# Two projection units on the unnormalised input, with the root put to them when they leave PSUM

## The reference

```python
xf = xf * lax.rsqrt(jnp.mean(xf * xf, axis=-1, keepdims=True) + EPS)   # rmsnorm
xn = (xf * g)
proj = xn @ w_in
q, k, v, u, gates = jnp.split(proj, splits, axis=-1)
...
bu = einsum('blgc,gpc->blgp', u, bb)        # state-space layer on u: a scan over the tokens
y = C x + d_skip * u
```

## Time and profile before

| | before |
|---|---|
| median of 3 runs | 1391.95 us (1390.6 to 1392.52) |
| the profiled execution | 1393.16 us |
| its span, first to last instruction | 1391.3 us |
| PE busy | 1369.7 us, 98% of the span |
| DVE, ACT, POOL busy | 49%, 60%, 15% |
| mean DMA rate | 182 GB/s |

### The profile page before, as it was taken

How to read it: one execution, slowest core, us unless ns; L and a number is a source line. 1 busy time by engine, 2 the same in 40 slices (tenths; PEclk the granted TensorE clock), 3 DMA queues, 4 the chain that set the end, 5 groups by cost and what they waited for, 6 DMA issues and landing times.

```text
span 1391.3 us, 18289 instructions
## 1 busy us (share of the span) xinstructions
PE 1369.7 (98%) x6634; PEld 1109.9 (80%) x6634; DVE 685.4 (49%) x1317; ACT 832.3 (60%) x1211; POOL 205.3 (15%) x240
## 2 busy tenths in 40 slices
PE   7999999999999999999999999999999999999998
PEld 4888877777788888888888887777798888888887
DVE  6993378988644445554154154745255301213324
ACT  7554877778665666665365366665667654535443
POOL 1111111100011111111111111110111111111112
PEclk9999999999999999999999999999999999999999
DMA  9998776676688888888878886755668898887973
GB/s 298 217 175 210 182 189 148 144 165 140 142 205 214 195 185 196 192 190 194 207 185 185 185 212 163 167 137 121 144 168 189 182 211 185 198 195 180 211 166 91
DMA packets 85670, 252.67 MB, mean 182 GB/s; under 512 B 16720, under 2 KB 24016, under 8 KB 85584
## 3 DMA queue, kind: packets, MB, share of 16 engines
q0 software_dynamic: 32400, 116.93, 46.8%
q1 hardware_dynamic: 51344, 131.06, 30.9%
q10 hardware_dynamic: 1840, 3.54, 0.7%
HBM read 126.98 MB, written 3.41 MB: 94 GB/s over the span
## 4 chain that ended last, share of the span: by engine, by line
PE 90%; DVE 5%; DMA 2%; ACT 2%; issue 1%; DVEq 0%; ACTq 0%
PE pg L646 26%; PE pg L648 25%; PE pg L647 25%; PE py L920 1%; PE ps L840 1%; PE ps L815 1%; PE ps L816 1%; PE ps L817 1%; DMA w_lo<-w_raw 1%; PE ps L1105 1%; PE ps L1113 1%; DMA act_lo<-w_raw 1%; DVE pairs L1842 1%; PE py L1123 1%; DVE acc L1845 0%
## 5 line engine op out<-in xcount | busy, mean ns | idle before, releaser
L646 PE MATMUL pg<-x_hi,w_hi 128*128 128x512 f32 x1008 | 397.5, 394 | 1.3 <-DVE gates L1842 1.3
L648 PE MATMUL pg<-x_hi,w_lo 128*128 128x512 f32 x1008 | 392.6, 390 | 0.0
L647 PE MATMUL pg<-x_lo,w_hi 128*128 128x512 f32 x1008 | 392.4, 389 | 0.0
L604 POOL DMA_DIRECT2D w_lo<-w_raw x221 | 190.9, 864 | 1144.5 <-ACT w_lo L1236 1068.3
L1235 ACT ACTIVATE w_hi<-w_raw 128x1024 fp32r<-128x1024 f32 (+1 forms) x215 | 224.4, 1044 | 108.9 <-PE pg L648 92.6
L646 PEld LDWEIGHTS pg<-x_hi,w_hi 128*128 128x128 f32 x1008 | 189.2, 188 | 49.9 <-issue 11.9
L1236 ACT ACTIVATE w_lo<-w_raw 128x1024 fp32r<-128x1024 f32 (+1 forms) x215 | 223.2, 1038 | 0.0
L648 PEld LDWEIGHTS pg<-x_hi,w_lo 128*128 128x128 f32 x1008 | 189.2, 188 | 39.9
L647 PEld LDWEIGHTS pg<-x_lo,w_hi 128*128 128x128 f32 x1008 | 189.3, 188 | 39.3 <-issue 1.0
L646 PE MATMUL pg<-act_hi,w_hi 128*128 128x512 f32 x424 | 164.9, 389 | 0.0
L647 PE MATMUL pg<-act_lo,w_hi 128*128 128x512 f32 x424 | 164.9, 389 | 0.0
(11 more groups left out here) (457 smaller groups left out, 1923.3 us busy)
## 6 DMA issues: line engine op xcount, KB each, us to landing
w_raw<-weights SPq DMA_DIRECT2D x218, 512.0 KB, 4.8
w_lo<-w_raw POOLq DMA_DIRECT2D x213, 512.0 KB, 5.6
kq_rot<-kq_raw SPq DMA_DIRECT2D x64, 64.0 KB, 2.4
w_raw<-weights SPq DMA_DIRECT2D x8, 384.0 KB, 4.3
w_lo<-w_raw POOLq DMA_DIRECT2D x8, 384.0 KB, 4.7
hid<-x SPq DMA_DIRECT2D x4, 512.0 KB, 5.6
hid<-x ACTq DMA_DIRECT2D x8, 256.0 KB, 5.0
act_lo<-w_raw POOLq DMA_DIRECT2D x4, 512.0 KB, 7.9
```

The source lines that it names most:

```text
L604: pool.dma_start(low_of(u)[:, 0:n], w_raw[:, s, 0:n], accum_op=ALU.add).then_inc(lo_in[s], 16)
L646: pe.matmul(bank[:], wh, xh(k), start=n == 0, stop=False)
L647: pe.matmul(bank[:], wh, xl(k), start=False, stop=False)
L648: last = pe.matmul(bank[:], wl, xh(k), start=False, stop=n == len(ks) - 1)
```

## The change

Units 0 and 1 are multiplied with the halves of x times norm weight, without the root (`raw_hi` by ACT, `raw_lo` by DVE), as each tile of x lands; the sum of squares runs on PE between and behind unit 0's products. The root is multiplied to the two outputs by DVE when they leave PSUM, in place of ACT's copies. Units 2 and 3 run side by side on the normalised halves, in two other PSUM banks, with the low products of unit 1 and 2 in between; ACT copies them out. Unit 0's weights are loaded first, x tile by tile behind them, the parameters on ACT's queue. Fourteen small products on a constant stand ahead of everything on PE. `into_turns` moves from behind gates 2 and 3 to behind gates 4 and 5, `kernels` from gate 4 to 7, `chunk_inputs` from gate 5 to 8; the first keys go ahead of `chunk_outputs`, the first queries ahead of `output_turns`. POOL's filling of `toep` moves behind two more weight units, and ACT's copies of `gt` follow the new places.

```diff
-FIRST_ON_PE, FIRST_ADDS = 3, 3
+FIRST_ON_PE, FIRST_ADDS = 2, 4
+WARM = 14
...
 # SP
-            for n in range(4):
-                sp.dma_start(hid[:, 2 * n:2 * n + 2], x_dram[:, 2 * n:2 * n + 2]).then_inc(x_landed[n], 16)
-            sp.dma_start(prm[:], params).then_inc(p_landed, 16)
             weights_to(0)
+            for k in range(KT):
+                sp.dma_start(hid[:, k], x_dram[:, k]).then_inc(x_landed[k], 16)
             weights_to(1)
+            weights_to(2)
             sp.dma_start(cst[:], consts[:, 0:C_ROT]).then_inc(c_landed, 16)
-            weights_to(2)
             weights_to(3)
...
 # PE
+            def input_units():
+                pe.wait_ge(ones_made, 1)
+                for n in range(WARM):
+                    pe.matmul(ps[0][:, 0, 0:P], ones_first, ones_first, start=True, stop=True)
                 pe.wait_ge(lo_first, 1)
                 for k in range(KT):
+                    pe.wait_ge(raw_low, k + 1)
+                    high(0, k, pg[0][:], raw_hi, raw_lo)
+                    low(0, k, pg[0][:], raw_hi)
+                    n = k - 3
+                    if 0 <= n < FIRST_ON_PE:
+                        pe.wait_ge(sq_done, n + 1)
+                        pe.matmul(px[:], ones_first, sq_first[:, n], start=n == 0, stop=False)
+                pe.wait_ge(sq_read, FIRST_ADDS)
+                pe.matmul(px[:], ones_first, sq_sum[1][:], start=False, stop=False)
+                pe.wait_ge(sq_done, KT)
+                pe.matmul(px[:], ones_first, sq_first[:, KT - 1], start=False, stop=True).then_inc(px_full, 1)
+                pe.wait_ge(hi_second, 1)
+                for k in range(KT):
+                    high(1, k, pg[1][:], raw_hi, raw_lo)
...
+                for k in range(KT):
                     pe.wait_ge(xlo_done, SPLIT["norm1"] + k + 1)
+                    for u in (2, 3):
+                        if k == 0:
+                            pe.wait_ge(hi_second, u)
+                        high(u, k, u_bank[u], x_hi, x_lo)
+                    if k == 1:
+                        pe.wait_ge(lo_in[1], lows(1))
+                    if 1 <= k < 5:
+                        low(1, 2 * k - 2, pg[1][:], raw_hi)
+                        low(1, 2 * k - 1, pg[1][:], raw_hi)
+                    if k == 5:
+                        pe.wait_ge(lo_in[2], lows(2))
+                    if 5 <= k < 7:
+                        low(2, 2 * k - 10, u_bank[2], x_hi)
+                        low(2, 2 * k - 9, u_bank[2], x_hi)
+                for k in range(4, KT):
+                    low(2, k, u_bank[2], x_hi)
+                pe.wait_ge(lo_in[3], lows(3))
+                for k in range(KT):
+                    low(3, k, u_bank[3], x_hi)
...
-            behind = {2: [lambda: into_turns(0)], 3: [lambda: into_turns(1)], 4: [kernels], 5: [chunk_inputs]}
-            first_pair()
+            behind = {4: [lambda: into_turns(0)], 5: [lambda: into_turns(1)], 7: [kernels], 8: [chunk_inputs]}
+            input_units()
             input_turns()
-            for t in range(2, SSM_T):
-                named(("u", t), XH, XL)
...
             values(0)
+            named(("k", 0), XH, XL)
             chunk_outputs(0)
             chunk_outputs(1)
-            named(("k", 0), XH, XL)
+            named(("q", 0), XH, XL)
             output_turns(0)
             output_turns(1)
-            named(("q", 0), XH, XL)
...
 # ACT
+            act.dma_start(prm[:], params).then_inc(p_landed, 16)
             ln_and_exp()
+            put(high_only(0), hi_done)
+            act.wait_ge(p_landed, 16)
             for k in range(KT):
-                act.wait_ge(x_landed[k // 2], 16)
+                act.wait_ge(x_landed[k], 16)
+                put(act.activation(raw_hi[:, k], hid[:, k], ACT.Copy, scale=par("norm1", k)), raw_high)
                 put(act.activation(sq_first[:, k], hid[:, k], ACT.Square), sq_done)
+                if k == 5:
+                    put(high_only(1), hi_second)
...
+            negated(1)
+            put(high_only(2), hi_second)
             act.wait_ge(ones_made, 2)
             inverse_root(1, rstd)
             for k in range(KT):
                 split_hi("norm1", k, x_hi[:, k], nrm[:, k % 2])
...
+                if k == 6:
+                    parts = hi_parts(("gate", GATES_FIRST[1]))
+                    next(parts)
+            next(parts)
             put(act.activation(lane[:, L_TANH], lane[:, L_Z], ACT.Tanh, scale=0.5), lane_act)
...
 # DVE
+            dve.tensor_tensor(w_lo[:, 0], w_raw[:, 0], w_hi[:, 0].bitcast(F32), ALU.subtract).then_inc(lo_first, 1)
             dve.wait_ge(p_landed, 16)
+            for k in range(KT):
+                if k == KT - 1:
+                    first_square(k - 1)
+                dve.wait_ge(raw_high, k + 1)
+                stt(raw_lo[:, k], hid[:, k], par("norm1", k), raw_hi[:, k].bitcast(F32), ALU.mult, ALU.subtract).then_inc(raw_low, 1)
+                if FIRST_ON_PE + 1 <= k - 1 < KT - 2:
+                    first_square(k - 1)
...
+            for t in range(2):
+                free(tt_(hid[:, t].rearrange("p (s c) -> p s c", c=NCH), done(("u", t)).rearrange("p (c s) -> p s c", s=STEP),
+                         rstd[:].rearrange("p (c s) -> p s c", s=STEP)), ("u", t))
```

More of the change, by code:

```diff
@@ L144, in in_pg @@
     o = TILE[name]
-    return o - sum(GROUP for h in (0, GROUP) if TILE[("v", h)] < o)
+    return o - 2 * (o > TILE[("u", 3)]) - sum(GROUP for h in (0, GROUP) if TILE[("v", h)] < o)
 SPLIT = {}
@@ L611, in _ @@
             pool.memset(toep[:], 0.0).then_inc(toep_zero, 1)
-            for v in range(11, len(UNITS)):
+            for v in range(13, len(UNITS)):
                 lo(v, v % RING)
@@ L652, in named, with high, low @@
                 tile(UNIT[name], name, xh, xl, **kw)
-            def first_pair():
-                def low(k):
-                    return pe.matmul(pg[1][:], w_lo[:, 1, k, :], x_hi[:, k], start=False, stop=k == KT - 1)
+            def input_units():
+                def high(u, k, bank, xh, xl):
+                    pe.matmul(bank, w_hi[:, u, k, :], xh[:, k], start=k == 0, stop=False)
+                    pe.matmul(bank, w_hi[:, u, k, :], xl[:, k], start=False, stop=False)
+                def low(u, k, bank, xh):
+                    last = pe.matmul(bank, w_lo[:, u, k, :], xh[:, k], start=False, stop=k == KT - 1)
+                    if k == KT - 1:
+                        last.then_inc(tile_done, 1)
+                pe.wait_ge(ones_made, 1)
+                for n in range(WARM):
+                    pe.matmul(ps[0][:, 0, 0:P], ones_first, ones_first, start=True, stop=True)
@@ L667, in first_pair @@
-                    if k == 0:
-                        pe.wait_ge(hi_second, 1)
-                    pe.matmul(pg[1][:], w_hi[:, 1, k, :], x_hi[:, k], start=k == 0, stop=False)
-                    pe.matmul(pg[1][:], w_hi[:, 1, k, :], x_lo[:, k], start=False, stop=False)
-                    if k == 5:
-                        pe.wait_ge(lo_in[1], lows(1))
-                        low(0)
-                    if k == 6:
-                        low(1)
-                        low(2)
-                for k in range(3, KT):
-                    last = low(k)
@@ L742, in into_turns @@
             def into_turns(half):
+                if half == 0:
+                    pe.wait_ge(u_copied, 2)
                 for r in range(2):
@@ L1296, in inverse_root, with high_only, negated @@
                 put(act.activation(dst[:], dst[:], ACT.Exp, scale=power), rstd_ready)
+            def high_only(u):
+                act.wait_ge(w_landed[u], 16)
+                return act.activation(w_hi[:, u], w_raw[:, u], ACT.Copy)
+            def negated(u):
+                put(act.activation(w_lo[:, u], w_raw[:, u], ACT.Copy, scale=-1.0), hi_done)
+            act.dma_start(prm[:], params).then_inc(p_landed, 16)
             ln_and_exp()
+            put(high_only(0), hi_done)
+            act.wait_ge(p_landed, 16)
@@ L1314, in _ @@
             for k in range(KT):
                 split_hi("norm1", k, x_hi[:, k], nrm[:, k % 2])
-                if k in (0, 2, 4):
-                    u = k // 2 + 1
-                    put(act.activation(w_lo[:, u], w_raw[:, u], ACT.Copy, scale=-1.0), hi_done)
-                if k in (1, 3):
-                    u = k // 2 + 2
-                    act.wait_ge(w_landed[u], 16)
-                    act.activation(w_hi[:, u], w_raw[:, u], ACT.Copy)
-                if k == 4:
+                if k == 0:
+                    put(high_only(3), hi_second)
@@ L1324, in _ @@
+                if k == 1:
+                    negated(2)
+                if k == 2:
+                    negated(3)
+                if k == 3:
+                    act.wait_ge(lane_dve, 1)
+                    put(act.activation(lane[:, L_MAG], lane[:, L_Z], ACT.Exp), lane_act)
+                    put(act.activation(lcf[:, 1], lcf[:, 0], ACT.Exp, scale=-1.0), lane_act)
                     act.wait_ge(c_landed, 16)
```

(12 more changed lines are left out.)

72 lines of the change are left out of this document (32 added, 40 removed).

## The result

The changed kernel takes 1400.91 us (median of 5 runs, 1398.04 to 1402.29) against 1392.52 (1390.6 to 1393.09) for the kernel before, run beside it: ratio 1.0058, 95% interval 1.0041 to 1.0074, that is 8.4 us slower. The forecast was 1395.0, slower, with a range up to 1399.0: the sign was right, the size was not.

What follows compares the result with a forecast made beforehand. PE, busy 98% of the span, was taken as the bound. Unit 16 starting 1.35 us later plus 1.7 of half clock made +3.05 on the 1391.95 median: 1395.0 us, range 1388.8 to 1399.0.

Steps and rivals of the forecast that it cites:

- The start: Up to the first gate: root 6.45 us later, logarithm at 19.7, first gate at 37.8 instead of 41.96, PE 4.1 ahead.
- rival 3: At the start: sparse products run at 1.2 GHz, root and all behind it about 2 us later, 1398.5; chance 0.13.
- The lane chain: DVE's state-space chain starts at 36.75, 7.3 us later, with its evictions and small copies just hidden (uncovered, up to 1.5).
- 0 to 2 us: Small stall at the turns, ACT held by unit 11's weights while PE wants their bank; only shortens the unit 16 wait.
- Moving the product three gates back covers DVE's delay there, and likewise the chunk inputs.: At the state-space products between PE's gates: the later places cover DVE's 7.3 us lateness, so no wait was counted.
- other orders: Behind unit 16: same products reordered (key unit, chunk outputs, query unit, transposes), none late: 0 us (-0.3 to +1).
- Unit 16: Last of the four value units: weights late behind toep in SP's queue, PE waits 6.7 us, starts 119.7, 1.35 later.
- The clock: Behind the 6.7 us wait at unit 16: 3.4 us at half clock, adding 1.7 us (0 to 3.4).
- The sum: Whole kernel: +1.35 for unit 16's later start and +1.7 for the clock make +3.05 us, giving 1395.0.

Runs made afterwards that it cites:

- stores_first: Changed kernel with SP's four stores of u issued ahead of the loads of units 8 to 10: 1399.20 us, ratio 1.0053 to the kernel before.
- keys_first: all_three plus the first key unit ahead of the values and unit 17's load between kt's store and toep: 1391.94 us, ratio 0.9997.
- evictions: Changed kernel with DVE's two root products in other layouts and two added SBUF products; profiled once, not timed: rows 0.69 us, 1.15 by steps in SBUF.
- rows_later: Changed kernel with only the loads of units 11 and 12 sent ahead of u_rows by SP: 1396.04 us, ratio 1.0025 to the kernel before.
- moves_alone: Kernel before, old start kept, with only the change's moved products, unit orders and matching ACT and POOL copies: 1397.34 us, ratio 1.0032.
- unit16_first: Changed kernel with unit 16's weight load issued by SP ahead of kt's store: 1399.18 us, ratio 1.0051 to the kernel before.
- all_three: Changed kernel with the edits of stores_first, places_earlier and unit16_first together: 1397.58 us, ratio 1.0043 to the kernel before.
- places_earlier: Changed kernel with kernels moved to behind gate 6 and chunk_inputs to behind gate 7: 1400.23 us, ratio 1.0051 to the kernel before.

## Why the prediction was wrong

**The start** was right in kind and 2.1 us too good. ACT began on the first weights at 5.20 (5.2 forecast), and in this trace the clock held through the sparse products. That was luck in part. In three of the other twelve traces with the new start it fell to 0.50 for 3.4 us: in stores_first from 8.3, at no cost that shows, in keys_first and evictions from about 17.6, where the last low half of x began at 35.0 instead of 32.9 to 33.9 and the first gate at 40.5. Those two are rival 3. A scaled copy costs ACT 0.61 net and not 0.52, so the pace was 1.13 per tile (6.17 to 7.30), and the logarithm came at 20.42 instead of 19.7. ACT waited 0.4 for PE to release a weight slot ahead of its last high half, the last low half ended at 34.4 instead of 33.25, and the first gate waited 0.5 for its low half, which took 8.5 us to land. First gate 39.95 instead of 37.8.

**The lane chain**: forecast 36.75, "just hidden" behind ACT's sines; it was 38.69, and DVE's own work was last there (sines done at 37.8): 1.15 from the later x and 0.95 from the evictions, the row above, over the 36.6 at which the forecast had DVE's own work end.

**The step that failed first** is the sentence that ACT held by the weights of unit 11 costs "0 to 2 us" and "only shortens that wait". It cost 3.9 and 1.7 of clock in the profiled execution. I had named the mechanism and not its size: u_rows and the store ahead of it stand in SP's queue too, and the load behind them moved from 59.2 to 67.6. The bound of 2 came from no row. And it could shorten the later wait only if unit 16's data stayed where they were; but they hang on kt, kt hangs on PE's product, and PE ran that product 7.8 us late, 2.1 from the start and the rest from this stall (95.91 for kt's store, where 88.9 follows from the forecast). rows_later takes this one step away, and there the forecast nearly comes out: POOL's issue for unit 16 at 115.54 (113.3), that unit at 120.19 (119.7), and 3.3 us over the kernel before (3.05), though the lead is spent in two waits there, 2.7 at the values and 1.0 at unit 16.

**The second step that failed**: "Moving the product three gates back covers DVE's delay there, and likewise the chunk inputs." A move back covers who feeds the step, and uncovers who reads it. Behind the ninth gate the chunk inputs have no product left between them and the values, which need their banks. moves_alone shows it without any lateness: 2.6 us, the clock, and 4.6 in all. The forecast's own numbers held it: 89.91 and 7.3 put DVE's read at 97.2, PE leaves the chunk inputs at 96.5, so the values would wait about 3 us (an estimate), and the sum has no such term. In the same way, moving the queries ahead of the output turns took the cover from the second values (0.9), where I wrote 0 (-0.3 to +1) for "other orders".

**Unit 16**, the centre of the forecast, was late as said, and later: POOL's issue at 120.47 (113.3 forecast), landing in 4.6 instead of 6.3, first product at 125.12 (119.7). But PE had lost its lead on the way, so the wait was 1.45 and not 6.7. Taken away by itself (unit16_first) it gives little: the lead that it spent was spent before.

```profile
120.47 0.86 POOL L613 DMA_DIRECT2D w_lo<-w_raw  x1 [19.78 <-ACT w_lo L1262]
```

**The clock**: that a wait is followed by half clock for 3.4 us, 1.7 lost, held, at another wait; behind the 1.45 at unit 16 it stayed at 1.00. The Trainium skill, TensorE: Matmul & The Clock Gate, Part 1, where the throttled clock is the default that activity releases, agrees with the 0.50 behind the wait at the turns.

**The sum** had one wait, of 6.7; the trace has four in a row, each of which PE meets with what the one before left.

## What to carry to other kernels

When a product is moved back to give its feeder time, look for the next user of its PSUM bank, and count the products left in between; when a store moves, list what its queue sends behind it and who on ACT stands first in line for that. A lead on PE is kept only if every wait behind it is covered: cover (a unit into another bank) was worth 5.6 us here, bringing DVE to its read 1.5 us earlier was worth 4. A wait that ends in a bank held by another engine may be two waits: read what that engine itself stood at. ACT stood at weights, DVE at PE's own product. When work moves on POOL, look at what DVE does beside its new place.

## What the runs showed of the hardware

- A DVE product of 128x512 in fp32 takes 0.69 us from PSUM, in plain order and by steps of eight elements, and from SBUF in plain order, but 1.15 by steps in SBUF (evictions). The Trainium skill, SBUF — State Buffer, in the section Door 1: The DMA port swizzle, says that SBUF is read in lines of 16 bytes and that crossing to a new line at each access is paid for; a step of 32 bytes agrees with that. For PSUM it has smaller lines and a slowdown of matmuls; DVE showed none.
- While POOL filled toep, one DVE instruction of 128x16 took 2.26 us instead of 0.17 and ended when POOL did; the tensor products beside it kept their times. In eleven other traces an instruction of this kind ended 0.02 to 0.03 us behind the filling in the same way (0.96 us in the kernel before, 0.50 in rows_later, 3.52 in stores_first). In the changed kernel this cost nothing, as DVE then stood at kt. These rows of after:

```profile
83.72 3.53 POOL L620 MEMSET toep<- 128x4096 f32 x1 [1.29 <-ACT e_sb L1398]
...
85.01 2.26 DVE L1892 TENSOR_SCALAR lane<-lane 128x16 f32<-128x16 f32 x1
```

- A stretch at 0.50 lasted 3.4 or 6.8 us in these traces. One followed the waits of 2.65 us in moves_alone, 2.7 in rows_later, 4.2 in all_three and 2.1 at the turns and 4.9 at unit 16 in places_earlier, yet none followed the 2.65 at the values in the changed kernel. Between 0 and 5.9 us of it lay in the products behind the wait, so such a wait cost up to 3.0 us more than itself (an estimate, half of the stretch).
